# Two neighbouring rows per partition in the down pieces of an expert layer, and gate and up columns read in steps of two

## The reference, cut to what matters

```
D_MODEL, SEQ, D_FF, N_EXPERTS, TOP_K = 1024, 256, 3584, 8, 2
logits = xt @ w_router                       # each token takes its two best experts
...
def expert_block(args):
    tok, e = args
    xb = xt[tok]
    return (silu(xb @ w_gate[e]) * (xb @ w_up[e])) @ w_down[e]
...
contrib = y_rows[pos] * gates[:, None]
y = segment_sum(contrib, flat_tok, num_segments=n_tok)
```

## Time and profile before

| | |
|---|---|
| median of 3 runs | 1380.4 us |
| the profiled execution's own time | 1378.5 us |
| its span in the trace | 1376.7 us |
| TensorE clock granted, mean | 0.997 of 2.4 GHz |
| TensorE busy (share of the span) | 1326.5 us (96%) |
| VectorE, ScalarE, GpSimd busy | 439.6, 325.8, 30.1 us |
| loads from HBM | 435.18 MB, mean 317 GB/s over the span |
| the eight expert items | 511.5 us to about 1366 us |

### The profile page before, as it was taken

The page is one execution under the profiler, slowest core; times in us unless marked ns, Lnnn a source line. Parts: engine busy times, 40 slices in busy tenths (PEclk is TensorE's granted clock), DMA queues, the critical chain, the costliest instruction groups (busy, mean ns, idle before and its releaser), DMA issues.

```text
span 1376.7 us, 31861 instructions
## 1 busy us (share of the span) xinstructions
PE 1326.5 (96%) x14177; PEld 796.7 (58%) x14177; DVE 439.6 (32%) x759; ACT 325.8 (24%) x526; POOL 30.1 (2%) x42
## 2 busy tenths in 40 slices
PE   6999999999999999999979999999999999999975
PEld 6987888888898974354333353354354345345332
DVE  4656655555578672201101101101101100110102
ACT  4645545544556842000000000000000000000001
POOL 2000000000011300000000000000000000000000
PEclk9999999999999999999999999999999999999998
DMA  9733555555453458999999999999999999999994
GB/s 293 273 123 127 194 184 186 196 195 188 127 164 123 153 217 335 374 413 418 413 412 419 414 410 420 415 410 419 416 408 419 416 395 418 417 401 417 418 408 187
DMA packets 133038, 438.34 MB, mean 318 GB/s; under 512 B 10690, under 2 KB 64160, under 8 KB 116512
## 3 DMA queue, kind: packets, MB, share of 16 engines
q1 hardware_dynamic: 131824, 433.27, 81.1%
q0 software_dynamic: 1072, 2.98, 0.7%
HBM read 435.18 MB, written 1.05 MB: 317 GB/s over the span
## 4 chain that ended last, share of the span: by engine, by line
PE 87%; DMA 7%; DVE 3%; SPq 2%; issue 1%; ACT 1%; POOL 0%; DVEq 0%
PE bank L1388 37%; PE bank L1409 16%; PE bank L1153 7%; PE bank L903 6%; PE bank L905 5%; PE bank L904 5%; DMA ring<-in_moe_w_down 4%; PE bank L1154 4%; DMA ring<-in_moe_w_gate 1%; DMA raw<-in_ev_w_in 1%; SPq L799 1%; PE bank L1440 1%; PE bank L1156 1%; PE bank L1460 1%; DVE arena L2170 0%
## 5 line engine op out<-in xcount | busy, mean ns | idle before, releaser
L1388 PE MATMUL bank<-ring,arena 128*32 128x512 f32 (+1 forms) x5632 | 537.3, 540 | 4.4 <-DMA ring<-in_moe_w_up 3.1
L1388 PEld LDWEIGHTS bank<-ring,arena 128*32 128x32 f32 x5632 | 179.6, 110 | 340.5 <-issue 323.6
L1409 PE MATMUL bank<-ring,arena 128*32 128x256 f32 x4928 | 272.4, 379 | 16.7 <-DMA ring<-in_moe_w_down 15.6
L1409 PEld LDWEIGHTS bank<-ring,arena 128*32 128x32 f32 x4928 | 158.2, 110 | 131.3 <-DMA ring<-in_moe_w_down 23.3
L702 DVE TENSOR_TENSOR low<-raw,high 128x2048 fp32r<-128x2048 f32 x73 | 167.3, 2294 | 83.5 <-ACT high L697 83.4
L697 ACT ACTIVATE high<-raw 128x2048 fp32r<-128x2048 f32 x73 | 139.3, 1910 | 53.3 <-PE bank L905 43.4
L1153 PE MATMUL bank<-ht_both,high 128*128 128x512 f32 x392 | 140.6, 398 | 0.6 <-DVE ht_both L1929 0.6
L2477 DVE TENSOR_TENSOR expert_rows<-expert_rows,bank 128x512 f32<-128x512 f32 (+1 forms) x44 | 27.3, 621 | 317.0 <-issue 163.0
L1154 PE MATMUL bank<-ht_both,low 128*128 128x256 f32 x448 | 116.6, 281 | 0.0
L1816 ACT ACTIVATE expert_rows<-bank 128x512 f32<-128x512 f32 (+1 forms) x44 | 23.7, 544 | 388.6 <-PE bank L1388 388.6
L1827 ACT ACTIVATE y_h<-bank 128x256 fp32r<-128x256 f32 x22 | 8.4, 383 | 396.8 <-PE bank L1409 396.8
(11 more groups left out here) (328 smaller groups left out, 1169.1 us busy)
## 6 DMA issues: line engine op xcount, KB each, us to landing
ring<-in_moe_w_down SPq DMA_DIRECT2D x112, 1024.0 KB, 18.7
ring<-in_moe_w_gate SPq DMA_DIRECT2D x64, 1024.0 KB, 19.4
ring<-in_moe_w_up SPq DMA_DIRECT2D x64, 1024.0 KB, 23.2
ring<-in_moe_w_gate SPq DMA_DIRECT2D x64, 768.0 KB, 20.8
ring<-in_moe_w_up SPq DMA_DIRECT2D x64, 768.0 KB, 20.6
raw<-in_ffn_w_gate SPq DMA_DIRECT2D x14, 1024.0 KB, 5.0
raw<-in_ffn_w_up SPq DMA_DIRECT2D x14, 1024.0 KB, 5.0
raw<-in_ffn_w_down SPq DMA_DIRECT2D x14, 1024.0 KB, 4.9
```

The lines of the kernel that those rows point to most:

```text
L1388: ins = mm(ps(use)[q * GRP:(q + 1) * GRP, 0:width], rows[:, k, r * GRP:(r + 1) * GRP], weights[:, q, :, :], start=k == 0, stop=k == DK - 1)
L1409: ins = mm(ps(use)[q * GRP:(q + 1) * GRP, 0:DN], m_act_t[:, r, first + c, :], ring[:, at + c * DM + q * DN:at + c * DM + (q + 1) * DN], st ...
```

## The change

A down piece is now 256 consecutive rows, taken as 128 pairs: partition p gets rows 2p and 2p+1 of the piece, which are one run of 8192 bytes in HBM and one in the ring. Block c of the down product is then the rows 2p + c. For the activations to match, the gate and up products read the weight columns in another order: of each 256 hidden columns, quarter q takes the 64 columns q*64 to q*64+63, first the even ones (c = 0), then the odd ones (c = 1), in steps of two elements. After the 32 x 32 turn, partition q*32 + i of block 2m + c holds hidden column 256m + 2(32q + i) + c, which is row 2p + c of piece m. Number and size of all instructions stay, and so do the number, the bytes and the order of the DMAs; the gate and up pieces are loaded as before.

```diff
@@ expert_piece (SyncE)
                 if kind == "d":
-                    first = PARTS[part][0] // P + 2 * k
-                    return dst.rearrange("p (k f) -> p k f", k=2), columns(wt, 0, first, first + 2, DM)
+                    first = PARTS[part][0] + 2 * P * k
+                    return dst, wt[first:first + 2 * P, :].rearrange("(p c) f -> p (c f)", c=2)
                 return dst.rearrange("p (k f) -> p k f", k=1), columns(wt, PARTS[part][0], k, k + 1, PARTS[part][1])
@@ expert_gate_up (TensorE)
-                weights = ring[:, at:at + NQ * width].rearrange("p (b q i) -> p q b i", q=NQ, i=GRP)
+                weights = ring[:, at:at + NQ * width].rearrange("p (m q i c) -> p q m c i", q=NQ, i=GRP, c=2)
...
                         ins = mm(ps(use)[q * GRP:(q + 1) * GRP, 0:width], rows[:, k, r * GRP:(r + 1) * GRP],
-                                 weights[:, q, :, :], start=k == 0, stop=k == DK - 1)
+                                 weights[:, q, :, :, :], start=k == 0, stop=k == DK - 1)
```

## The result

The changed kernel takes 1391.66 us at the median of four runs (1389.62 to 1393.43), the kernel before 1380.28 us beside it: a ratio of 1.0081, 95% interval 1.0064 to 1.0098. It is slower by 11 us, where 8.7 us less was forecast. The execution profiled after took 1393.43 us, 1391.6 us of it span.

What follows compares the result with a forecast made beforehand. The end of the loads was taken to set the end, though TensorE bounds the middle. Profiled 1378.5 us less 8.7 for down loads, nothing for other terms, gives 1369.8, plus 1.9 to the median: 1371.7 us; 8-in-10 range 1368 to 1381.

Steps and rivals of the forecast that it cites:

- The loads: Down pieces, all 112 moved after 560 us: 0.078 us less each from fewer, longer rows, 8.7 us in all.
- reading of the chain: Waits are on the DMA to about 718 us, on TensorE to about 1307 us, then on the DMA to the end.
- rivals 2: Down loads: 407 GB/s not due to row count, so 0 to a third of 8.7 us comes; 1379 us, chance 0.14.
- rival 3: Ring of 14 places: the loads' lead cannot grow, only 2.2 us before 718 us come; 1378.2 us, chance 0.07.
- 4 (slower reading of neighbouring rows): Down loads from HBM: rows at a pitch of 8192 bytes read 2% slower, 5.9 us more, 1386.3 us; chance 0.02.
- The gate and up products: Line 1388 on TensorE: reading in steps of two was taken to cost nothing; at half pace 537.3 us would double.
- sign of being wrong: Line 1388: busy time growing by more than 7 us in the stretch TensorE bounds would show the prediction wrong.
- Rival 1: Gate and up products: steps of two slow TensorE; no gain at 3.8%, 0.2% slower at 4.5%, 1897 us at half pace; chance 0.11.
- own sum: Rival 1's pricing: 416.1 us of gate and up products, each per cent beyond 1.8% adding 4.2 us.
- 7.3 us of room: Item 7: TensorE idle time left, 13.8 us less the 6.5 us asked for; up to 1.8% slower products cost nothing.
- The queued work: DMA queue in the TensorE-bound middle: some 15 us of loads queued, over twice the 6.5 us of lead needed.

Runs made afterwards that it cites:

- the shape experiment: Against the kernel before, loads unchanged: gate products read in three nested loops with unit steps, up products in steps of two in one long run; 1383.49 us in one run.

## Why the prediction was wrong

**The loads: right.** 128 rows fewer for each down piece: the queue has 131824 - 117488 = 14336 packets less by its two profiles, 112 x 128. The rate of the down stretches is 419 to 420 GB/s, the issue on SyncE 333 ns at the median. Alone they make the kernel 0.59% faster, 8.2 us (8.7 between the medians); 8.7 were worked out. The reading of the chain is right too: with the loads alone the end of the loads sets the end. Of the gain, 3.0 us show at the hand-over (715.79 against 718.83 us for the first product of item 2) and 5.4 in item 7 (85.3 us to its last product in place of 90.7), where 2.2 and 6.5 were expected. For the loads alone that leaves rivals 2 (at most a third of the gain), 3 (only the part ahead of 718 us) and 4 (slower reading of neighbouring rows) without support; the limit of rival 3, the 14 places of the ring, comes in once TensorE is slower (below).

**The gate and up products: the step that failed.** The prediction put this term at nothing, "as the row nearest to it, with its jumps, shows nothing". That row had jumps between runs, and no step inside a run; it could not bound the step, and the shape experiment shows that the two are different things. The term is 5.8 to 6.1% of line 1388 in the bound stretch: 21.7 us there by the two groups (221.8 + 165.2 against 209.6 + 155.7), 29.6 us over the span. The prediction's own sign of being wrong was 7 us in the bound stretch. The rule of the Trainium skill that the prediction weighed beside it (Advanced Engine Details and Errata, SBUF Cachelines), by which a step of two float32 elements reads at full pace, errs by this much here; that a step with one hit a line costs more, the trace bears out, with 2.1 times.

**Rival 1 was the case, with a cost between its ends.** The prediction said that such a cost, if it exists, was likely well above 4.5%; it is 6%, little above the point from which the kernel is slower. With 5.9% its own sum gives 416.1 x 0.059 = 24.6 us, less 7.3 us of room: 1371.7 + 17.2 = 1388.9 us. Measured 1391.7. What is missing is not the price but what was taken for free. From the profile of the loads alone to that of the whole change (1370.12 to 1393.43 us, 23.3 us):
- the expert items begin at 514.3 us in place of 511.3: 3.0 us. No code in that part was changed. The granted clock was 0.81 and 0.85 in 120 to 130 and 130 to 140 us of this profile and 1.00 in that of the loads alone, and the longest product of line 1153 there took 767 ns in place of 467. So it is the clock of this one execution, and no part of the change.
- the hand-over to TensorE: 730.57 against 722.30 us, 8.3 us, 5.3 of it new. The prediction took items 0 and 1 for free. They are not, as the kernel with steps outside items 2 to 6 shows with 5.1 us.
- from there to the start of item 7: 1298.05 - 730.57 against 1268.98 - 722.30, 20.8 us for the five items. The sum has 365.3 x 0.059 = 21.6.
- item 7 gives back 29.1 - 23.4 = 5.7 us (last product at 1377.66 against 1354.28). The sum has 7.3 us of room less 3.0 of dearer products, 4.3, so item 7 gave more than it was asked for.

Leaving out the first, that is 20.4 us where the sum has 17.3, and the 5.3 us of items 0 and 1 are more than the whole difference. In item 7 TensorE's waits, first with the loads alone (1269 to 1358 us), then with the whole change (1298 to 1382 us), were

```profile
L1409 PE MATMUL bank<-ring,arena 128*32 128x256 f32 x449 | 28.7, 400 | 8.3 <-DMA ring<-in_moe_w_down 7.1 <-issue 1.0
```
```profile
L1409 PE MATMUL bank<-ring,arena 128*32 128x256 f32 x448 | 25.7, 380 | 2.8 <-DMA ring<-in_moe_w_down 2.8
```

5.5 us of idle time used and 2.8 left. The down products also took 3.0 us less, since in the loads alone the granted clock fell to 0.83 from 1340 to 1350 us; the two together are the 5.7 us and the 2.8 us that item 7's own gate and up products cost more.

**The queued work was no cover for this.** The prediction read 15 us of queued loads as room for a greater lead, and for the loads alone that was nearly right: 5.4 of 6.5 us came. With TensorE 20 us slower the lead is bound by the 14 places of the ring: hence the stretches at 366 GB/s, and hence an item 7 in which loads, though faster, are again the last to come.

What stays open is why a step of two costs 6%, and what the four streams share. The runs say that it is not the loads' writes, nor restarts, nor the number of loops, and that one stepping stream is enough.

## What to carry to other kernels

Where two resources are within 5% of each other (here 110.69 us of TensorE for an item beside 44.04 MB at 413 GB/s, 106.6 us of loads), a change that helps one by a little at the cost of an untried form on the other should be priced at that form first, by the form alone: a row that resembles it in another respect is no bound. A new order of data need not be paid on the engine that sets the pace; the one with idle time, here VectorE at 32% busy, can make it as it writes. Idle time behind a wait for loads is no room for the engine if the loads in turn wait for places that this engine frees.

## What the runs showed of the hardware

- A moving operand of float32 in steps of two elements costs 6% over unit steps (0.0860 against 0.0811 us for 384 columns), whether the inner run restarts every 32 elements or never (0.1153 and 0.1155 us for 512 columns); in steps of four or eight 2.1 times (0.2295 and 0.2322 us for 512 columns against 0.1095). Loads at 57 GB/s or at 402 beside it make no difference (0.1166 and 0.1153 us).
- Four column groups of which one or two read in steps of two are slower (0.122 us for 512 columns) than four that all do (0.1157).
- An estimate: a DMA row costs about 9.7 ns of its engine beside its bytes, by a straight line through 407, 415.5 and 419.7 GB/s for rows of 4096, 6144 and 8192 bytes, and 419 to 420 GB/s for the down weights once their rows had 8192.
- With 128 rows in place of 256 the issue of a 1 MB load held SyncE for 333 ns at the median in place of 2084.
